# Modulation steps moved into the first projection, and two expert chunks loaded into freed attention space

## The reference, cut to what matters

```
mod = s_c @ ada_w[l] + ada_b[l]                     # 1024 -> 6 * 1024, for c and for c_ctx
sh1, sc1, g1, sh2, sc2, g2 = split(mod, 6)
hx = rms_norm(x, norm1_g[l]) * (1 + sc1) + sh1      # needs sh1, sc1
y  = token_mixers(hx, hc, w_in[l], w_out[l], ...)   # gating, Fourier, two attentions
x  = x + g1 * y
h  = rms_norm(x, norm2_g[l]) * (1 + sc2) + sh2
x  = x + g2 * expert_choice_ffn(h, router_w[l], wg, wu, wd)
```

## Time and profile before the change

| | us |
|---|---|
| runs: median (lowest to highest) | 2337.89 (2337.7 to 2343.71) |
| profiled execution: span of its core (the only time given for it) | 2346.5 |
| busy: TensorE, its weight load | 2140.5, 1483.4 |
| busy: VectorE, ScalarE, GpSimd | 1132.2, 844.9, 44.2 |
| moved by DMA | 660.95 MB, mean 282 GB/s |
| mean granted clock of TensorE | 0.971 of full speed |

### The profile page before, as it was taken

How to read it: one execution, slowest core, us unless ns; L and a number is a source line. 1 busy time by engine, 2 the same in 40 slices (tenths; PEclk the granted TensorE clock), 3 DMA queues, 4 the chain that set the end, 5 groups by cost and what they waited for, 6 DMA issues and landing times.

```text
span 2346.5 us, 33361 instructions
## 1 busy us (share of the span) xinstructions
PE 2140.5 (91%) x14368; PEld 1483.4 (63%) x14368; DVE 1132.2 (48%) x1775; ACT 844.9 (36%) x1258; POOL 44.2 (2%) x76
## 2 busy tenths in 40 slices
PE   9999999989898999966565789999999999999998
PEld 5866743423232777533232348888988888888887
DVE  5646531212121777310010138668877677568765
ACT  4436321111111556200000025445655455456544
POOL 0022000000000011000000000000000000000000
PEclk9999999999999999988888899999999999999999
DMA  8375679999999553999999994454554544364442
GB/s 347 120 318 246 257 310 425 427 427 428 428 427 426 201 224 140 377 427 426 428 427 427 426 407 182 149 210 171 189 190 159 195 180 180 135 234 180 157 172 88
DMA packets 66978, 660.95 MB, mean 282 GB/s; under 512 B 7504, under 2 KB 10576, under 8 KB 21136
## 3 DMA queue, kind: packets, MB, share of 16 engines
q1 hardware_dynamic: 66832, 658.83, 69.3%
HBM read 657.76 MB, written 1.05 MB: 281 GB/s over the span
## 4 chain that ended last, share of the span: by engine, by line
PE 69%; DMA 24%; DVE 3%; ACT 2%; issue 1%; SPq 0%; DVEq 0%; ACTq 0%
PE ps L967 21%; PE ps L1460 11%; PE ps L968 10%; DMA ring_top<-in_exp_up 9%; DMA ring_top<-in_exp_down 5%; PE ps L937 5%; PE ps L938 5%; PE ps L939 5%; DMA ring_top<-in_exp_gate 4%; DMA ring<-in_exp_up 3%; PE ps L986 2%; DMA ring<-in_exp_down 1%; DMA ring<-in_ada_w 1%; PE ps L1154 1%; PE ps L1453 1%; PE ps L1417 1%
## 5 line engine op out<-in xcount | busy, mean ns | idle before, releaser
L967 PE MATMUL ps<-h_buf_r,ring_r 128*128 128x512 f32 x800 | 283.8, 399 | 1.5 <-DVE h_buf_r L759 1.5
L1460 PE MATMUL ps<-ring,arena 128*32 128x256 f32 (+1 forms) x1632 | 215.0, 514 | 67.3 <-DMA ring<-in_exp_up 38.0
L2787 DVE TENSOR_TENSOR h_buf<-h_buf,ps 128x512 f32<-128x512 f32 (+1 forms) x32 | 17.8, 555 | 490.0 <-PE ps L1460 478.1
L968 PE MATMUL ps<-h_buf_r,ring_r 128*128 128x256 f32 x800 | 224.7, 281 | 0.0
L967 PE MATMUL ps<-h_buf_r,ring_top_r 128*128 128x512 f32 x608 | 217.4, 402 | 2.9 <-DVE h_buf_r L759 2.9
L1460 PE MATMUL ps<-ring_top,arena 128*32 128x256 f32 (+1 forms) x1328 | 164.2, 512 | 59.5 <-DMA ring_top<-in_exp_up 29.0
L1460 PEld LDWEIGHTS ps<-ring,arena 128*32 128x32 f32 (+1 forms) x1632 | 80.1, 132 | 199.0 <-issue 109.5
L485 DVE TENSOR_TENSOR ring_r<-ring,ring_r 128x2048 fp32r<-128x2048 f32 (+4 forms) x92 | 177.7, 1967 | 50.6 <-ACT ring_r L477 50.5
L967 PEld LDWEIGHTS ps<-h_buf_r,ring_r 128*128 128x128 f32 x800 | 150.3, 188 | 39.2 <-issue 1.9
L968 PE MATMUL ps<-h_buf_r,ring_top_r 128*128 128x256 f32 x608 | 171.4, 282 | 0.0
L1460 PEld LDWEIGHTS ps<-ring_top,arena 128*32 128x32 f32 (+1 forms) x1328 | 61.9, 133 | 159.1 <-issue 84.6
(11 more groups left out here) (390 smaller groups left out, 4144.7 us busy)
## 6 DMA issues: line engine op xcount, KB each, us to landing
ring<-in_exp_gate SPq DMA_DIRECT2D x35, 2048.0 KB, 28.2
ring<-in_exp_down SPq DMA_DIRECT2D x35, 2048.0 KB, 30.5
ring<-in_exp_up SPq DMA_DIRECT2D x34, 2048.0 KB, 30.2
ring_top<-in_exp_gate SPq DMA_DIRECT2D x29, 2048.0 KB, 29.1
ring<-in_ffn_w SPq DMA_DIRECT2D x50, 1024.0 KB, 6.9
ring_top<-in_exp_up SPq DMA_DIRECT2D x24, 2048.0 KB, 30.7
ring_top<-in_exp_down SPq DMA_DIRECT2D x24, 2048.0 KB, 28.3
ring_top<-in_ffn_w SPq DMA_DIRECT2D x38, 1024.0 KB, 6.9
```

The source lines that it names most:

```text
L967: release(pe.matmul(ps[:, bank, :], w[0][:, lo:lo + P], both, start=start, stop=False, skip_group_check=True))
L968: return pe.matmul(ps[:, bank, 0:N], w[1][:, lo:lo + P], both[:, 0:N], start=False, stop=stop, skip_group_check=True)
L1460: mm = pe.matmul(out, stationary, slot(c)[:, at:at + width], start=start, stop=stop)
```

## The change

Modulation steps 1 and 2 now stand in the first projection: quarters 0 and 1 of step 1 behind the jobs of chunk 0, quarters 2 and 3 behind chunk 1, those of step 2 behind chunks 2 and 3; the turns stand behind the first job of chunks 2 and 4. The last two groups of products of step 0 are separated by a group of the projection. Step 3 stands behind spatial gating, 4 and 5 in the neighbourhood attention. The start of that attention has no step. In the route, 8, 6, 4 and 2 products of zeros stand where step 5 was. The stream has the weights in this order, and chunks 1 and 2 of expert 0 have homes, loaded when the neighbourhood attention is done.

```diff
         HOMES = {
+            ("experts", 0, 1): [part(8192, 10240), part(14336, 16384)],
             ("experts", 0, 2): [part(10240, 14336)],
-            ("ada", 5, 3): [part(8192, 10240), part(14336, 16384)],
...
             if l == 0:
                 stream(("ada", 0), *[PLAIN] * 4)
-            stream(("w_in", l), HALVED, HALVED, HALVED, (2, SLOT), (1, KT * GROUP))
-            if l == 0:
-                for step in range(1, 5):
+                for c in range(4):
+                    stream(("w_in", 0, c), w_in_chunks[c])
+                    stream(("ada_pair", 1 + c // 2, c % 2), PLAIN, PLAIN)
+                stream(("w_in", 0, 4), w_in_chunks[4])
+                for step in range(3, 6):
                     stream(("ada", step), *[PLAIN] * 4)
...
             stream(("w_out", l), HALVED, HALVED)
-            if l == 0:
-                stream(("ada", 5), *[PLAIN] * 4)
...
                 if l == 0:
                     first_pair(0, range(0, 4))
-                    for c in range(2):
-                        first_ada_products(1, c)
-                    first_pair(1, range(0, 2))
+                    first_ada_products(1, 0)
+                    first_pair(1, (0,))
+                    first_ada_products(1, 1)
+                    first_pair(1, (1,))
                     first_ada_turn(1)
...
                     owed[0] += 1
+                    ada_products(1, (0, 1))
                     j = 4
...
                     if c not in [a[0] for a in jobs[j:]]:
                         owed[0] += 1
+                        if l == 0 and c in (1, 2, 3):
+                            ada_products(1 + c // 2, (2, 3) if c % 2 else (0, 1))
+                    elif l == 0 and t == 0 and c in (2, 4):
+                        ada_turn(c // 2)
...
                 d_scores(l, 1)
                 if l == 0:
                     pe.wait_ge(sem("c_out"), 4)
-                    ada_products(2)
...
-                        ada_products(3 + i // 4, (i % 4,))
+                        ada_products(4 + i // 4, (i % 4,))
...
                 if l == 0:
-                    ada_products(5, (0,))
+                    stay_busy(3, 8)
...
-                    ada_products(5, (1,))
+                    stay_busy(3, 6)
                     for j in range(turned_first(l), 8):
                         pe.wait_ge(sem("h_tok"), j - 4)
                         turn_tokens(l, j)
+                    stay_busy(3, 4)
...
-                if l == 0:
-                    ada_products(5, (2,))
-                else:
-                    stay_busy(3, 2)
+                stay_busy(3, 2)
                 pe.wait_ge(sem("h_tok"), 2 * tiles + before("h_tok", l))
                 pick_products(l, 0)
                 pick_turns(l, 0)
-                if l == 0:
-                    ada_products(5, (3,))
...
-                            if l == e == which == 0 and k == 3:
-                                ada_turn(5)
...
                 if l == 0:
-                    ada_products(1)
+                    ada_products(3)
                 fourier_channels(l)
                 if l == 0:
-                    ada_turn(1)
+                    ada_turn(3)
...
                     halve_lead(act, w_in(l, 2))
                     projection(l, (1,))
+                    ada_group(1)
...
                 gate_stats(l)
+                if l == 0:
+                    ada_group(2)
                 projection(l, (4,))
...
-                halve_rest(dve, n + 2)
-                halve_rest(dve, n + 3)
+                halve_rest(dve, w_in(l, 2))
+                if l == 0:
+                    ada_group(1)
+                halve_rest(dve, w_in(l, 3))
...
                     for c in range(6):
+                        if l == e == 0 and c == 5:
+                            sp.wait_ge(sem("d_pv"), len(units(0)))
+                            load_expert_home(0, 1)
+                            load_expert_home(0, 2)
```

More of the change, by code:

```diff
@@ L406, in build, with w_in, ada_chunk @@
             stream(("ple", l), HALVED, HALVED)
+        def w_in(l, c):
+            return chunk_at["w_in", l, c]
+        def ada_chunk(step, i):
+            return chunk_at["ada_pair", step, i // 2] + i % 2 if step in (1, 2) else chunk_at["ada", step] + i
         def expert_chunk(l, e):
@@ L572, in load_expert_home, with ada @@
                           P * SLOT * (2 * (EXPERTS * l + e) + which % 2), pieces)
-            def ada(step):
-                first = read_to.get("ada_w", 0)
-                for j in range(4):
-                    if chunk_at["ada", step] + j in home_of:
-                        read_to["ada_w"] += P * SLOT
-                    else:
-                        load(chunk_at["ada", step] + j, "ada_w", SLOT)
-                if step == 5:
-                    sp.wait_ge(sem("d_pv"), len(units(0)))
-                    load_expert_home(0, 2)
-                    load_home("ada", 5, 3, "ada_w", first + 3 * P * SLOT)
+            def ada(step, pieces=range(4)):
+                for i in pieces:
+                    load(ada_chunk(step, i), "ada_w", SLOT)
             def ffn(i):
@@ L616, in _ @@
                     load(chunk_at["w_out", l] + i, "w_out", SLOT)
-                if l == 0:
-                    for step in range(5, 6):
-                        ada(step)
                 for e in range(EXPERTS):
                     for c in range(6):
+                        if l == e == 0 and c == 5:
+                            sp.wait_ge(sem("d_pv"), len(units(0)))
+                            load_expert_home(0, 1)
+                            load_expert_home(0, 2)
                         if l and e == 0 and c == 4:
@@ L978, in ada_products @@
                     pe.wait_ge(sem("ada_mod"), step + 1)
-                for k in (2 * i + half for i in pieces for half in range(2)):
-                    if k % 2 == 0:
-                        chunk(n + k // 2)
-                    for j in range(4):
-                        at = 2048 * (k % 2) + 512 * j
-                        c = n + k // 2
-                        w = HOMES[home_of[c]][k % 2][:, 512 * j:512 * j + 512] if c in home_of else slot(c)[:, at:at + 512]
-                        mm = pe.matmul(ps[32 * j:32 * j + 32, ada_bank(step), :], cond[:, k, :], w, start=k == 0, stop=k == KT - 1)
-                        if k == 0 and j == 0:
+                for i in pieces:
+                    n = ada_chunk(step, i)
+                    chunk(n)
+                    for k in (2 * i, 2 * i + 1):
+                        for j in range(4):
+                            at = 2048 * (k % 2) + 512 * j
+                            mm = pe.matmul(ps[32 * j:32 * j + 32, 7, :], cond[:, k, :], slot(n)[:, at:at + 512],
+                                           start=k == 0, stop=k == KT - 1)
                             release(mm)
-                    if k % 2:
-                        mm.then_inc(weights_used, 1)
+                    mm.then_inc(weights_used, 1)
             def first_ada_products(half, c):
-                n = chunk_at["ada", 0] + 2 * half + c
+                n = ada_chunk(0, 2 * half + c)
                 if half == c == 0:
@@ L1854, in ada_group @@
             def ada_group(step):
-                act.wait_ge(weights_used, chunk_at["ada", step] + 4)
-                act.activation(ada_rows(step), ps[:, ada_bank(step), :], ACT.Copy).then_inc(sem("ada_rows"), 1)
+                act.wait_ge(weights_used, ada_chunk(step, 3) + 1)
+                act.activation(ada_rows(), ps[:, 7, :], ACT.Copy).then_inc(sem("ada_rows"), 1)
             def first_ada(half):
-                act.wait_ge(weights_used, chunk_at["ada", 0] + 2 * half + 2)
+                act.wait_ge(weights_used, ada_chunk(0, 2 * half + 1) + 1)
                 own = slice(256 * half, 256 * half + 256)
-                act.activation(ada_rows(0)[:, own], ps[:, 7, own], ACT.Copy).then_inc(sem("ada_rows"), 1)
+                act.activation(ada_rows()[:, own], ps[:, 7, own], ACT.Copy).then_inc(sem("ada_rows"), 1)
             def projection(l, chunks, tiles=range(4)):
```

126 lines of the change are left out of this document (60 added, 66 removed).

## The result

The changed kernel took 2353.2 us in the median (2339.9 to 2358.51, 11 runs), the kernel before 2339.15 on the same chip (2336.58 to 2348.23). The medians lie 14 us apart, the means (2351.1 and 2341.2) 9.9. The ratio that is used here agrees with the means: 1.0042, with a 95% interval of 1.0029 to 1.0056, so the change costs about 9.8 us (6.8 to 13.1). The forecast was 5.5 us, with rival A at 10.5.

A forecast was written before the change was run, and what follows sets the result against it. TensorE was taken to bound up to 346.99, then the expert transfers, ending 423 us later. Terms +14.0, +0.9, -1.4, +1.0, -6.7, -1.7, -0.6 sum to +5.5 on 2337.9: 2343.4 us, range 2335 to 2350.

The forecast's parts named there:

- rival A: Projection, chunk 3's third job: late weights put each us straight onto the path; 5 us more gives +10.5, 2348.4; chance 0.18.
- The likeliest case: Whole kernel: the forecast case, +2 to +9 us, 2340 to 2347; chance 0.60.
- Two steps in the projection: First projection: steps 1 and 2 lie on the path in full, 2 x 7.0, +14.0 us; bounds 13.5 to 14.5.
- Two turns: First projection: turns 1 and 2, four transposes each taking 0.43, now stand there; +0.9 us.
- Start: Step 0's last quarter: first-pair products before it cover its 1.42 wait for weights; -1.4 us, bounds -1.5 to 0.
- Stall: Projection, chunk 3's third job: waits for ScalarE's read of chunk 2, held by chunk 4's load; +1.0 us, bounds 0 to 6.
- the opposite of B: A fall of the granted clock at a new place; +7.3 us, 2345.2.
- Attention's start: Neighbourhood attention's start: without step 2 the first turn waits only for the exponentials; -6.7 us, bounds -7.0 to -4.
- Route: Route: step 5's third and fourth quarters leave the path, fillers stand there instead; -1.7 us, bounds -3.5 to -1.
- rival B's rise: Route: the new row at full clock gives 1.3 us more, and the stall may be nil; +3.2, 2341.1; chance 0.12.
- Step 5's turn: Behind the first expert product: the turn of step 5, 0.59 at 326.76, goes; -0.6 us.
- Rival C: Experts' stage: earlier loads start the saturated stretch sooner, its end coming down by 34 us to 2309; chance 0.10.

The follow-up runs named there:

- w4_first: The changed kernel with the load of the projection's chunk 4 issued before the last two quarters of step 2; ratio 1.0034 to the kernel before.
- before_split: The kernel before, with a group of first-pair products put between the last two quarters of step 0; ratio 0.9990.
- fill_wait: The changed kernel with 16 filler products ahead of the third job of the projection's chunk 3; ratio 1.0041 to the kernel before.
- homes_7_14: The changed kernel with projection chunk 4 loaded first and early-loaded homes for expert 1's chunk 1 and expert 2's chunk 2 instead; 2338.17 us, ratio 0.9982.
- before_homes: The kernel before with step 0's quarters split, and homes for expert 1's chunks 2 and 3 replacing expert 0's chunk 2 and step 5's last quarter; ratio 1.0020.
- no_homes: The changed kernel with chunks 1 and 2 of expert 0 loaded through the ring instead of into attention space; ratio 1.0052 to the kernel before.
- homes_8_9: The changed kernel with homes for chunks 2 and 3 of expert 1 instead of chunks 1 and 2 of expert 0; ratio 1.0050 to the kernel before.

## Why the prediction came out as it did

The range of 2335 to 2350 holds the time that the ratio gives, 2337.89 x 1.0042 = 2347.7, but not the changed kernel's own median of 2353.2. The likeliest case did not come: the price is A's, 10 us, and of the three outcomes it is "slower", which had 0.38. Term by term, from one execution of each kernel:

1. **Two steps in the projection**, forecast +14.0: +15.1. From its first product to the projection's next half a step takes 3.57; its first product comes 0.32 behind the one before it and the second product of the projection 0.34 behind its first, where 0.227 is usual. So each half step costs 3.57 + 0.1 + 0.1 = 3.77, four of them 15.1. The bound of 14.5 was too low. w4_first, without any gap, has +15.0 at the projection's end, and 15.1 + 0.9 - 1.0 gives that.
2. **Two turns**, +0.9: 2 x (0.35 + 0.1) = +0.9.
3. **Start**, -1.4: -1.0 in this run, -1.5 in before_split.
4. **Stall**, +1.0: this is the step that failed. The mechanism was right in each link, but the gap is 124.92 - 121.1 = 3.8, and the clock's fall behind it adds 2.6: +6.4. The text had the load issued at 105.6 and down at 115. It was issued behind the quarter's load of 107.6, at 107.97 (chunk 2 was done 1.2 us later than forecast, and the queue went on only when the half step behind it had run for 1 us), and down at 119.13. So the first of the two loads went out 2.0 late and the data took 2.1 longer from there; the third job was due 1.3 later than forecast, which gives that much back: 2.0 + 2.1 - 1.3 = 2.8 us more. Rival A priced just this ("each us goes straight onto the path"); w4_first bears it out, and fill_wait shows the second price. In the other four kernels with this projection the term is 4.2 to 6.1 instead of 6.4, still far from 1.0. The bounds of 0 to 6 held the gap, and the clock's fall stood among the rivals as the opposite of B; that both come together, the one by the other, was not put together. The Trainium skill, TensorE: Matmul & The Clock Gate, What's actually happening, says that the default state is throttled and that activity releases the throttle. By that rule a gap can bring a second price, and the trace agrees with 0.50 behind 3.8 us of gap and 1.00 where fillers stood in it; not every gap does, as behind the 1.21 us ahead of the first expert product the clock stayed at 1.00.
5. **Attention's start**, -6.7: 14.94 - 21.56 = -6.6. The turn waits 0.42 for ScalarE's exponentials, as named.
6. **Route**, -1.7: -3.9. This is rival B's rise, which was priced at 1.3 and brought 2.2: with the clock at 1.00 throughout, the first expert product comes 114.95 us behind the first turn, for 118.85 before. In the five kernels with fillers where the clock fell it is 115.8 to 117.3, so -3.1 to -1.6: the forecast's figure comes only with the deepest fall, that of homes_7_14. The kernel before had an expensive execution, too: before_split and before_homes, with the same route products, took 117.6 and 117.5.
7. **Step 5's turn**, -0.6: from +11.0 to +10.1, -0.9.

The measured terms sum to 15.1 + 0.9 - 1.0 + 6.4 - 6.6 - 3.9 - 0.9 = +10.0, for the 10.1 at the stage's end.

**Rival C** fell for this change: 422.8 us from expert 0's chunk 4 to the end, and no_homes shows that the two chunks in advance are worth 0.5 us. The prediction's own reason, that the end is fixed by the use of that chunk "whatever was loaded before", holds only while the queue pauses there: in no_homes it doesn't. And C's idea was not empty. The prediction argued that the earlier loads "only fill a ring that is full sooner". The homes for chunks 1 and 2 are used up before the pause; for chunks 7 and 14 the same amount of space is worth 9 us of the stage: from the first expert product to the product on the last load it is 766.86 - 329.49 = 437.4 us, against 773.97 - 327.66 = 446.3 in w4_first. What the text lacked was to ask which chunk's slot the load behind the pause waits for, and how to move that.

**Still open:** whether the fillers hold the route's clock, and why the total of w4_first lies near 8 us above the kernel before where the marks up to the stage's end give 4.0. A part may be chance of the two executions that were profiled. The clock fell in the route in all three other kernels with w4_first's projection (0.8 to 2.3 us more than in w4_first), and the kernel before had the slowest route of the three kernels that share it (by 1.2 to 1.3 us). With both, the marks would give up to 7.6; this is an estimate from those rows, not a measurement.

## What to carry to other kernels

When a step is moved in among dense work, look for the one load that its own loads are now queued ahead of, and follow that load through the in-order engine that waits for it; a swap of loads gave back 6 of the 10 us here, by the marks of one execution each. Count a gap of some us on TensorE twice where the granted clock is at its upper level: once for its length, and once for the products behind it (1.3 to 2.9 us here). Spare room for a prefetch ring is worth most for the chunks just behind the last wait on a slot, spread so that used slots keep coming free, and issued ahead of any load that waits.

## What the runs showed of the hardware that was not expected

- A gap of 3.8 us on TensorE brought the granted clock from 1.00 to 0.50, the level of 1.2 GHz, for about 5 us of dense products, and cost 2.6 us; fillers in the same gap kept it at 1.00. In six executions with gaps of 2.6 to 7.7 us the cost was 1.3 to 2.9 us, and it didn't follow the length of the gap.
- In the route the clock fell in some versions and not in others, though TensorE's work ahead of it is the same: from the attention's first turn to the first expert product it took 114.9 to 115.0 us in five kernels with the clock at 1.00, and 115.8 to 117.3 in the five (with fillers) in which it fell.
- Each half step between products of the projection cost 0.2 us beyond the 3.57 from its first product to the next of the projection's, at the seams ahead of it and behind it.
- A chunk of 2 MiB takes 4.97 us in an unbroken stretch, its start included, where the division by 427 GB/s had given 4.91: 4.965 over 85 chunks (358.0 to 780.06), 4.966 over 89 (homes_8_9), 4.975 over 87 (334.0 to 766.81, homes_7_14).
